# Twelve of eighteen modulation vectors moved from matmuls to VectorE, and an attention loop with three stages in flight

## The reference

```python
for layer in range(DEPTH_2):                     # 2 layers, N_MOD = 9
    mx = split(silu(c) @ ada_w[layer] + ada_b[layer], N_MOD)        # vectors of width 1024
    mc = split(silu(c_ctx) @ ada_w[layer] + ada_b[layer], N_MOD)
    x = x + 0.5 * mx[2] * swiglu(modulate(rms_norm(x), mx[0], mx[1]), ffn1...)
    # then the mixers (attention, pooling, Fourier) with mx[3], mx[4], mx[5]
    # then a second feed-forward with mx[6], mx[7], mx[8]; the context does the same with mc
```

## Time and profile before

| | |
|---|---|
| median of 3 runs | 2354.18 us (2352.47 to 2357.14) |
| the profiled execution's own time | 2349.65 us |
| its span, first to last instruction | 2347.9 us |
| mean granted TensorE clock | 0.989 of full speed |
| PE busy | 2275.5 us, 97% of the span |
| DVE / ACT / POOL busy | 1060.8 / 695.0 / 198.3 us |
| data moved | 407.8 MB, mean 174 GB/s |

### The profile page before, as it was taken

How to read it: one execution, slowest core, us unless ns; L and a number is a source line. 1 busy time by engine, 2 the same in 40 slices (tenths; PEclk the granted TensorE clock), 3 DMA queues, 4 the chain that set the end, 5 groups by cost and what they waited for, 6 DMA issues and landing times.

```text
span 2347.9 us, 32138 instructions
## 1 busy us (share of the span) xinstructions
PE 2275.5 (97%) x13844; PEld 1829.4 (78%) x13844; DVE 1060.8 (45%) x1626; ACT 695.0 (30%) x950; POOL 198.3 (8%) x195
## 2 busy tenths in 40 slices
PE   7999999999999999999999999999999999989998
PEld 6778975555478888899459888888888888848998
DVE  5676534333364333352446333335433334446554
ACT  5444331111142212232444221213212222344333
POOL 2111210000010000120112000012000003012002
PEclk9999998999999999999999999999999999999999
DMA  9775887999953243232843323323323323444573
GB/s 291 259 266 181 287 305 292 420 421 420 398 151 97 80 120 90 75 96 77 319 142 90 91 86 110 100 75 97 108 80 109 95 73 115 152 169 133 165 203 110
DMA packets 371515, 407.81 MB, mean 174 GB/s; under 512 B 10841, under 2 KB 342094, under 8 KB 350126
## 3 DMA queue, kind: packets, MB, share of 16 engines
q1 hardware_dynamic: 356174, 326.07, 42.2%
q0 software_dynamic: 14896, 79.09, 9.2%
q10 hardware_dynamic: 304, 0.59, 0.1%
HBM read 404.66 MB, written 1.05 MB: 173 GB/s over the span
## 4 chain that ended last, share of the span: by engine, by line
PE 86%; DVE 7%; ACT 3%; DMA 2%; issue 1%; SPq 0%; POOL 0%; DVEq 0%; ACTq 0%
PE B L1739 23%; PE B L1741 22%; PE B L1740 22%; PE B L2118 6%; PE B L2138 3%; PE B L2088 2%; DMA HF<-in_ada_w 2%; PE B L1860 2%; PE B L2076 2%; ACT T L1667 1%; DVE LO L669 1%; DVE SM L1232 1%; DVE R L680 1%; DVE HF L1025 1%; DVE T L1245 1%; DMA XS<-in_ctx 1%
## 5 line engine op out<-in xcount | busy, mean ns | idle before, releaser
L1739 PE MATMUL B<-hH,HI 128*128 128x512 f32 (+1 forms) x1936 | 659.1, 340 | 14.0 <-DVE hL L1013 7.0
L1740 PE MATMUL B<-hL,HI 128*128 128x512 f32 (+1 forms) x1936 | 653.8, 338 | 0.0
L1741 PE MATMUL B<-hH,LO 128*128 128x512 f32 (+1 forms) x1936 | 653.7, 338 | 0.0
L669 DVE TENSOR_TENSOR LO<-RAW,HI 128x2048 fp32r<-128x2048 f32 (+3 forms) x218 | 443.8, 2038 | 121.2 <-ACT HI L1323 111.4
L1323 ACT ACTIVATE HI<-RAW 128x2048 fp32r<-128x2048 f32 (+3 forms) x218 | 368.6, 1692 | 356.6 <-PE B L1741 276.8
L1739 PEld LDWEIGHTS B<-hH,HI 128*128 128x128 f32 x1936 | 368.8, 190 | 60.0 <-DVE LO L669 11.9
L1741 PEld LDWEIGHTS B<-hH,LO 128*128 128x128 f32 x1936 | 368.9, 191 | 39.4
L1740 PEld LDWEIGHTS B<-hL,HI 128*128 128x128 f32 x1936 | 369.0, 191 | 38.4 <-issue 0.2
L1124 DVE TENSOR_TENSOR T<-B,T 128x512 f32<-128x512 f32 (+1 forms) x88 | 55.0, 625 | 492.4 <-PE B L1741 492.4
L1741 PE MATMUL B<-aH,LO 128*128 128x512 f32 (+1 forms) x770 | 269.3, 350 | 0.0
L1739 PE MATMUL B<-aH,HI 128*128 128x512 f32 (+1 forms) x770 | 269.0, 349 | 0.0
(11 more groups left out here) (353 smaller groups left out, 2631.8 us busy)
## 6 DMA issues: line engine op xcount, KB each, us to landing
RAW<-in_ffn_w_gu SPq DMA_DIRECT2D x176, 512.0 KB, 5.0
W<-in_w SPq DMA_DIRECT2D x78, 1024.0 KB, 11.5
HF<-in_ada_w POOLq DMA_DIRECT2D x48, 1024.0 KB, 7.8
W2T<-in_w SPq DMA_DIRECT2D x39, 1024.0 KB, 11.9
RAW<-in_w_in SPq DMA_DIRECT2D x60, 512.0 KB, 5.0
RAW<-in_ffn_w_down SPq DMA_DIRECT2D x56, 384.0 KB, 3.7
RAW<-in_ffn_w_down SPq DMA_DIRECT2D x56, 320.0 KB, 4.2
ADW<-in_ada_w POOLq DMA_DIRECT2D x16, 1024.0 KB, 10.8
```

What stands on the lines that cost most here:

```text
L669: V.tensor_tensor(LO[s][:, :words], RAW[s][:, :words], HI[t.hi[s]][:, :words].bitcast(F32), ALU.subtract).then_inc(lo_done[s], 1)
L1739: mm(o, wh, xh, start=first, stop=False, **more)
L1740: mm(o, wh, xl, start=False, stop=False, **more)
L1741: return mm(o, wl, xh, start=False, stop=last, **more)
```

## The change

- **Layer 0, vectors 0 to 5** stay on PE: three full-width groups, 24 units. Eight stand in the projections, two in each of heads 0 to 3, none in heads 4 to 7, none in `w_out`, and four in each of the two calls in the expert choice, now of full width.
- **The other twelve vectors** (`MOD_PLAN`) go to DVE in three of the four feed-forward stages, four to a stage. A unit is now 128x1024 (0.5 MB, `mod_weights` on POOL, two places MADW). `mod_sum` does a unit with two DVE instructions of 128x1024, one for each input: MACC[v] = MADW * c + MACC[v]. When eight units are done, MACC still has 128 partial sums for each column; PE adds them with eight matmuls (`mod_sums`, `PICK` as weights, 256 columns, in four column tiles), ACT copies, PE turns the result with two matmuls of 8 columns (`mod_turn`), and DVE reads it (`mod_read`).
- In gate-and-up chunks 1 to 8 (first half) and 1 to 4 (second half) DVE does two units after its `prep`; in the first eight down chunks of the first half it does one.
- **No units in the mixers**: `FILL`, the unit in the attention loop and five `ada_finish` are gone.
- **The attention loop** has three stages in flight in place of two: PE does the transposes of u-3, scores(u), the value product of u-3; ACT does exp(u-1) in iteration u; DVE does maxima(u), then scales u-1, then splits u-3. Scores have four banks instead of three, probabilities six tiles instead of four, and `yf` stands inside iterations 0 and 1.
- POOL's table `pool_mix` is loaded twice (its place is shared with MADW).

```diff
+MOD_PLAN = [(0, m) for m in range(6, N_MOD)] + [(1, m) for m in range(N_MOD)]
+PLAN_PER_FFN = 4
+SUMS_AT = {(0, 5): 0, (0, 9): 1, (1, 0): 2, (1, 5): 3}
+TURN_AT = {(h, j + 1): g for (h, j), g in SUMS_AT.items()}
-ADA_GROUPS = [ADA_W] * 4 + [ADA_W // 2]
+ADA_GROUPS = [ADA_W] * 3
...
+            def mod_weights(n0, n1):                       # POOL
+                for n in range(n0, n1):
+                    (l, m), k = MOD_PLAN[n // KT], n % KT
+                    if n >= 2:
+                        pool.wait_ge(*mod_used(n - 2))
+                    pool.dma_start(MADW[n % 2][:], a["ada_w_2"][l][k * P:(k + 1) * P, MOD_W * m:MOD_W * (m + 1)])\
+                        .then_inc(ada_loaded[n % 2], 16)
...
+            def mod_sum(n):                                # DVE
+                k = n % KT
+                ve.wait_ge(ada_loaded[n % 2], 16 * mod_used(n)[1])
+                if n > 0:
+                    ve.wait_ge(*mod_used(n - 1))
+                if k == 0:
+                    ve.wait_ge(E["mod_summed"], n // KT)
+                for v in range(2):
+                    c = CS[:, k, v:v + 1]
+                    if k == 0:
+                        ins = V.tensor_scalar(MACC[v][:], MADW[n % 2][:], c, None, ALU.mult)
+                    else:
+                        ins = V.scalar_tensor_tensor(MACC[v][:], MADW[n % 2][:], c, MACC[v][:], ALU.mult, ALU.add)
+                ins.then_inc(ada_used[n % 2], 1)
...
+                        if f is not None and 1 <= j <= KT:  # DVE, gate-and-up chunk j, after prep
+                            q = PLAN_PER_FFN * f + 3 * half + (j - 1) // 4
+                            for k in range(2):
+                                if q < PLAN_PER_FFN * (f + 1):
+                                    mod_sum(KT * q + 2 * ((j - 1) % 4) + k)
...
+            def mod_sums(q):                               # PE
+                claim(6, "ada_copied", len(ADA_GROUPS) + q + 1)
+                pe.wait_ge(*mod_used(KT * (q + 1) - 1))
+                w = MOD_W // COL_TILES
+                for v in range(2):
+                    for j in range(COL_TILES):
+                        ins = mm(B[6][CT_W * j:CT_W * (j + 1), 0:w], PICK[:, v, :], MACC[v][:, w * j:w * (j + 1)],
+                                 start=(v == 0), stop=(v == 1))
+                ins.then_inc(E["mod_summed"], 1)
...
-                ada(HEAD_UNITS[h])
+                if h < 4:
+                    ada(2)
...
-                ada(2)                                     # PE, w_out, four times
...
-                ada(FILL[0])                               # PE, mixers, four places
...
+                    if u >= 3:                             # PE, attention loop
+                        h, q0, k0, nk = pairs[u - 3]
+                        got("prob_ready")
+                        for c in range(2):
+                            claim(2 + c, "probT_ready", before + 2 * (u - 3) + c + 1)
+                            for kb in range(nk // P):
+                                ins = nc.tensor.transpose(B[2 + c][:, kb * P:(kb + 1) * P],
+                                                          PROBS[2 * (u - 3) % 6 + c][:, kb * P:(kb + 1) * P], mat(IDENT))
+                            ins.then_inc(E["probT_done"], 1)
-                    if mix_finish(l, u) is not None:
-                        ada_finish(1, mix_finish(l, u))
-                    if mix_unit(l, u):
-                        ada(1)
```

More of the change, by code:

```diff
@@ L241, in build @@
         DFT = at(61, "DFT", [P, 2, TB, S])
+        MACC = [at(45 + 4 * v, f"MACC{v}", [P, MOD_W]) for v in range(2)]
+        MADW = [at(53 + 4 * i, f"MADW{i}", [P, MOD_W]) for i in range(2)]
         TRIG = at(65, "TRIG", [P, 2, S])
@@ L580, in ada_weights, with pool_tables @@
                         pool.wait_ge(ada_used[place], n // 4)
-                    rows = a["ada_w_2"][l][k * P:(k + 1) * P, c0:c0 + w]
-                    pool.dma_start(ADW[l][place][:, 0:w // S, :], rows.rearrange("p (b n) -> p b n", n=S))\
+                    rows = a["ada_w_2"][0][k * P:(k + 1) * P, c0:c0 + w]
+                    pool.dma_start(ADW[place][:, 0:w // S, :], rows.rearrange("p (b n) -> p b n", n=S))\
                         .then_inc(ada_loaded[place], 16)
+            def mod_weights(n0, n1):
[5 more added lines that the diff above has]
+                        .then_inc(ada_loaded[n % 2], 16)
+            def pool_tables(n):
+                for i in (1, 2):
+                    pool.wait_ge(*mod_used(n - i))
+                pool.dma_start(POOL[:], a["pool_mix"]).then_inc(E["mix_consts_loaded"], 16)
             def inputs_used():
@@ L1045, in _ @@
             select(1)
-            ada_read(0, 4)
+            ada_read(2)
             got("rows_ready")
@@ L1121, in ffn @@
                             prep(FFN_CHUNKS[j + 1])
+                        if planned(f, TURN_AT, half, j) is not None:
+                            mod_read(planned(f, TURN_AT, half, j))
+                        if f is not None and 1 <= j <= KT:
[3 more added lines that the diff above has]
+                                    mod_sum(KT * q + 2 * ((j - 1) % 4) + k)
                         products()
@@ L1132, in ffn @@
                             prep(words)
+                        if f is not None and half == 0 and i < KT:
+                            mod_sum(KT * (PLAN_PER_FFN * f + 2) + i)
                         products()
@@ L1221, in mixers @@
                     turned(4)
-                for d in range(2):
-                    mix_split(B[2 + d][:, :n], 6 + d, 0, P, 0, n)
                 pairs = attention_pairs(l)
-                for u in range(len(pairs) + 2):
+                for u in range(len(pairs) + 3):
                     i = 2 * u % 4
@@ L1532, in _, with ffn @@
             norm(0, 0, 0)
-            def ffn(n, more):
+            def ffn(n, more, f=None):
                 for half in range(2):
@@ L1539, in ffn @@
                             prep(FFN_CHUNKS[j + 1])
+                        if planned(f, SUMS_AT, half, j) is not None:
+                            mod_copy()
                         got("gate_done")
@@ L1863, in ada, with mod_turn @@
                 t.n["unit"] += count
+            def mod_sums(q):
+                claim(6, "ada_copied", len(ADA_GROUPS) + q + 1)
+                pe.wait_ge(*mod_used(KT * (q + 1) - 1))
+                w = MOD_W // COL_TILES
+                for v in range(2):
+                    for j in range(COL_TILES):
+                        ins = mm(B[6][CT_W * j:CT_W * (j + 1), 0:w], PICK[:, v, :], MACC[v][:, w * j:w * (j + 1)],
+                                 start=(v == 0), stop=(v == 1))
+                ins.then_inc(E["mod_summed"], 1)
+            def mod_turn():
+                got("ada_copied")
+                claim(7, "mod_read")
+                o = B[7][:, 0:2 * KT].rearrange("p (j c v) -> p j c v", j=COL_TILES, v=2)
+                for c in range(KT // COL_TILES):
+                    ins = mm(o[:, :, c, :], MADT[:, c * P:(c + 1) * P], ASEL[:].rearrange("p (j v) -> p j v", v=2),
+                             start=True, stop=True)
+                ins.then_inc(E["ada_done"], 1)
             for c in range(12):
@@ L2180, in into_ffn, with ffn @@
                             used(ins, slots[j])
-            def ffn(n, stagger):
+            def ffn(n, stagger, f=None):
                 for h in range(2):
                     for j in range(FT_HALF):
+                        if planned(f, TURN_AT, h, j) is not None:
+                            mod_turn()
+                        if planned(f, SUMS_AT, h, j) is not None:
+                            mod_sums(planned(f, SUMS_AT, h, j))
                         if h == 0 and j < 2:
@@ L2407, in mixers @@
                         ins.then_inc(E["scores_done"], 1)
-                    if u >= 2:
-                        h, q0, k0, nk = pairs[u - 2]
+                    if u < 2:
+                        pe.wait_ge(E["ft_ready"], t.n["ft_ready"])
+                        claim(2 + u, "mix_ready")
+                        for p in range(2):
+                            ins = mm(B[2 + u][:, :n], FW[:, l, p, u * P:(u + 1) * P], T[2 + p][:, :n], start=(p == 0),
+                                     stop=(p == 1))
+                        ins.then_inc(E["yf_done"], 1)
+                    if u >= 3:
+                        h, q0, k0, nk = pairs[u - 3]
                         pe.wait_ge(E["probT_ready"], t.next("probT_ready", 2))
```

206 lines of the change are left out of this document (97 added, 109 removed).

## The result

The changed kernel takes 2318.7 us (median of four runs, 2315.46 to 2319.05), the kernel before 2353.3 beside it: the ratio is 0.9849, with a 95% interval of 0.9832 to 0.9867. The forecast was 2317, in a range of 2300 to 2338. The profiled execution of the changed kernel took 2315.46 us; its span of 2313.7 is 34.2 shorter than that of before, and the forecast's sum was 36.7. So the total came out nearly as forecast; its terms didn't, as the stages show.

A forecast was written before the change was run, and what follows sets the result against it. PE, busy 97% of the span, was taken to bound the kernel nearly everywhere. Terms won 56.0 us and lost 19.3, net 36.7 off 2354.2, giving 2317.5 us; predicted 2317, range 2300 to 2338.

The forecast's parts named there:

- Feed-forward, PE's part: Feed-forward stages: `mod_sums` and `mod_turn` add 1.6 us of PE work twelve times, 19.3 us lost, bounds 15 and 24.
- rival A: Feed-forward gate-and-up chunks: DVE or its transfers become the bound, 36 chunks about 3 us late, 2425 us; chance 5%.
- Feed-forward, DVE's part: Feed-forward stages: 96 units, 236 us of DVE work, lie under PE and cost nothing; 1.7 us idle left per gate-and-up chunk.
- Transfers: Feed-forward units' 512 KB loads from POOL's queue: 8 us before DVE waits, 1.7 more before late; earlier ones took 4.6 and 6.9.
- Before the loops: Mixers ahead of the attention loops: removing eight units per layer wins 8.4 us in layer 0 and 11.4 in layer 1.
- The loops: Attention loops: iterations fall from 4.36 to 3.2 us (512 keys) and 3.13 to 2.2 (256); 16 and 8.6 us won.
- Heads 4 to 7: Head stage: eight units leave PE, but DVE's pace then limits the gain; 2.2 us won, bounds 0.9 and 7.4.
- rival C: Attention loop and heads 4 to 7: PE's clock falls where units are gone, giving back 29 us, 2346 us; chance 10%.
- `w_out` and the expert choice: `w_out`: eight units removed from PE, 7.4 us won; expert choice: eight half-width units become full-width, 2 us won, bounds -2 and +4.

The follow-up runs named there:

- three_banks: The changed kernel with three banks for the attention scores instead of four, the loop's new order kept: 2354.0 us, 1.0002 of the kernel before.
- old_loop: The changed kernel with the attention loop in its old order, three score banks and `yf` ahead, without units in it: 2355.3 us, 1.0011 of the kernel before.
- old_data: The changed kernel with the expert choice's last four units reading the previous four's data, without their own transfers (4 MB less): 2311.3 us, 0.9818 of the kernel before.

## Why the prediction was right, and where its steps weren't

- *Feed-forward, PE's part* (19.3 lost): 3 x 6.8 = 20.4. The mechanism and the size held; 1.70 for a vector instead of 1.6. (The forecast speaks of 24 gate chunks that would be late without cover; they are 12 in each of three stages, 36, as its rival A has it.)
- *Feed-forward, DVE's part* (nothing): right. The instruction took 1.279 us (1.28 estimated), 57% of the stage (58%), 1.82 us left before the product (1.7). A first unit's `tensor_scalar` took less than I gave it, 0.747 us. The Trainium skill has this in "VectorE: DVE Perf Modes", section "The perf-mode tier table (the rule you actually need)": with fp32 a single-source instruction such as `tensor_scalar` can run at twice the rate of one with two tensor operands. By that rule, the trace agrees in direction, with 1.7 times and not twice: 0.747 against 1.279.
- *Transfers*: half a MB landed 3.9 us after its issue at the median (4.6 and 6.9 in the earlier trace rows); DVE waited 3.5 us for them in all before its accumulating instructions. The first pairs of a stage came later than I had them, with no effect on PE.
- *Before the loops* (8.4 and 11.4): 28.8 - 20.2 = 8.6 and 23.0 - 10.7 = 12.3, the loops taken out.
- *The loops* (16 and 8.6): from the first scores at 1138.09 to the last split at 1186.45 it is 48.4 us where it was 68.6, 20.2 won; in layer 1 from 2046.90 to 2078.54, 31.6 against 42.3, 10.7 won. An iteration takes 3.11 (3.2 forecast) with 512 keys and about 2.0 (2.2) with 256, so the pace was close; the 3.9 us of layer 0 that were won beyond the sum lie in the first iterations after the fill (2.4 and 2.6 instead of 3.2), in those with 256 keys and in the drain. The forecast's reason had two parts, that the exponentials wait "for nothing of the same iteration" and that "the scores have a bank free". three_banks shows that the second can't be missing; that the first can't either is read from old_loop's rows and was not run, and neither was the new order with the units left in.
- *Heads 4 to 7* (2.2 won): 1.0 lost. The lead was there: the LO that stood at 207.72 came at 204.15, 3.6 us earlier, 0.7 of it from before the heads; the clock then took it back, 0.92 over the stretch instead of 0.97. In the three kernels without these units that also read 0.97, the stretch is 1.8 to 2.5 us shorter than before, which is the size forecast. What the sum lacked is rival C, in one of the places that I named and not in the others: the loop with PE at 94% kept 1.00. The Trainium skill, "TensorE: Matmul & The Clock Gate", section "HAM oscillation — how this bites in real kernels", has such falls after idle gaps of PE. The traces agree for the first fall in the heads and for the start of the old loop, where fillers in the gaps kept the clock at 1.00; the 2.70 us ahead of `w_out`, after which it fell in ten kernels and not in four, show that the gap alone doesn't decide it.
- *`w_out` and the expert choice* (7.4 and 2 won): 3.4 together over the second and third stretch. From the mark in `w_out` to the router's last matmul it is 31.8 us before and 23.5 after (the rows below), 8.2 won, so the `w_out` term held.

```profile
347.44 1.14 PE L2026 MATMUL B<-T,XC 128*128 128x128 f32 x8
...
341.93 1.14 PE L2104 MATMUL B<-T,XC 128*128 128x128 f32 x8
```

  The 2.4 us of the gate chunks (the clock's fall after 306 and the late transfer) stood in no term. The step that failed is the expert choice's: from there on 2.4 us were lost instead of 2 won. The forecast counted PE's matmuls into the wait and gave the last four units' 4 MB, "which can be sent only as the first four are used", no price within the 2. They cost 4.5 us (old_data).

So 9 us missed before the experts (11.6 forecast, 2.4 found) stand against 7 us more than forecast in the mixers (51.8 instead of 44.4). That the sum was right within 2.5 us is luck to that extent: the two misses have nothing to do with each other.

## What to carry to other kernels

Follow the waits of a loop twice: once for the chain that sets its pace now, and once for the one that would set it in the new order. Here the new order without a fourth score bank won nothing, and with it 35 us; the old order's rows show no wait that the bank alone would have ended. Work that lies in PE's waits wins nothing when it is taken out, and may have been what kept the clock up: read the clock after it, and try a few small matmuls in the gap, over more than one pair of kernels. Work put into a wait is only hidden if its transfers are too.

## What the runs showed of the hardware

- In the middle of old_loop's loop PE was busy 5.8 of 8 us in window after window and the clock stayed at 1.00, where in the heads a gap in its work was followed by the lower level. After one and the same wait of 2.70 us ahead of `w_out` it fell in ten kernels and not in four. And in the changed kernel it fell at 1083 us with no idle time of PE in the 8 us before it:

```profile
1075.00:1083.00 8.00, 8.00 (x74) 8.00 (x74) 0.00 (x0) 0.55 (x2) 0.00 (x0) 1.00 0.01 2
1083.00:1092.00 9.00, 9.00 (x52) 9.00 (x52) 1.99 (x1) 3.17 (x6) 0.00 (x0) 0.62 0.34 117
```

  So idle time alone doesn't tell where it falls. What does stays open.
- A set of eight column-tiled fp32 matmuls of 256 columns costs 1.07 us the first time and 0.87 when it follows its like.
- The lengths of FFN 1 agree within 0.1 us in eight kernels (374.4), while the stretches before the experts vary by 1 to 3 us between kernels with the same program there, and their granted clock with them (0.92 to 0.97 in the heads). Small differences are best read from a stage that repeats, with the clock beside them.
